# Two fused transformer layers: an order of transposes, late squares, and memory queries without their norm

## What is computed

```python
x = x + rmsnorm(y @ w_out, g_mix_post)
h = rmsnorm(x, g_mem_pre)
q = (h @ w_mq).reshape(B, S, MEM_HEADS, MEM_HEAD_DIM)      # 4 heads of 256
logits = einsum('bshd,bmhd->bhsm', q, k) * MEM_HEAD_DIM ** -0.5
p = softmax(logits); o = einsum('bhsm,bmhd->bshd', p, v)
x = x + rmsnorm(o @ w_mo, g_mem_post)
h = rmsnorm(x, g_ff_pre)
x = x + rmsnorm(square(relu(h @ w_ff1)) @ w_ff2, g_ff_post)
...
qkv = silu(causal_short_conv(g_qkv, conv_w)); gq, gk, gv = split(qkv)
gq = l2_normalize(gq) * 128 ** -0.5; gk = l2_normalize(gk)
o_gdn = gated_delta_rule_chunked(gq, gk, gv, g, beta)
x = x + (sigmoid(gate_a) * o_gdn + sigmoid(gate_b) * o_att) @ w_out_2
h2 = rms_norm(x, norm_mlp_g); x = x + square(relu(h2 @ w_mlp_up)) @ w_mlp_down
```

## Time and profile before

| | us |
|---|---|
| median of 3 runs | 990.76 (990.04 to 992.05) |
| the profiled execution | 989.58 |
| its span from first to last instruction | 987.8 |
| TensorE busy | 944.5 (96%) |
| VectorE busy | 590.7 (60%) |
| ScalarE busy | 526.6 (53%) |
| GpSimd busy | 120.1 (12%) |

### The profile page before, as it was taken

One profiled execution on the slowest core, in us unless ns is written; L12 is line 12 of the kernel. 1 busy time (PEld: TensorE's weight loads), 2 busy tenths in 40 slices (PEclk: granted clock), 3 DMA queues, 4 the chain that ended last, 5 costly groups with the idle time before them and its releaser, 6 DMA issues. The chain is left out here.

```text
span 987.8 us, 15123 instructions
## 1 busy us (share of the span) xinstructions
PE 944.5 (96%) x5920; PEld 831.3 (84%) x5920; DVE 590.7 (60%) x903; ACT 526.6 (53%) x949; POOL 120.1 (12%) x131
## 2 busy tenths in 40 slices
PE   5999999999999999998999998999999999999998
PEld 5996978788889988887779897887899779998886
DVE  4456556753766654446578988776446566665432
ACT  5555666654655453336477686753455364544331
POOL 0020000100100000001014222401654100000000
PEclk9999999999999999999999998999999999999999
DMA  9663423541556655554446443432110064655552
GB/s 339 235 194 129 128 89 126 179 144 41 170 176 191 210 172 197 186 171 171 133 135 203 128 147 110 129 127 86 44 43 2 29 216 150 195 181 174 207 173 85
DMA packets 99702, 146.74 MB, mean 149 GB/s; under 512 B 2480, under 2 KB 57904, under 8 KB 99504
## 3 DMA queue, kind: packets, MB, share of 16 engines
q1 hardware_dynamic: 99632, 145.78, 45.1%
HBM read 144.72 MB, written 1.05 MB: 148 GB/s over the span
## 5 line engine op out<-in xcount | busy, mean ns | idle before, releaser
L396 DVE TENSOR_TENSOR s_w_lo<-s_w_raw,s_w_hi 128x2048 fp32r<-128x2048 f32 (+1 forms) x198 | 313.2, 1599 | 195.7 <-ACT s_w_hi L390 195.7
L390 ACT ACTIVATE s_w_hi<-s_w_raw 128x2048 fp32r<-128x2048 f32 (+1 forms) x198 | 262.6, 1345 | 132.3 <-PE acc L448 103.6
L458 PE MATMUL acc<-s_h_hi,s_w_hi 128*128 128x256 f32 x800 | 228.3, 285 | 6.0 <-DVE s_w_lo L396 4.6
L459 PE MATMUL acc<-s_h_lo,s_w_hi 128*128 128x256 f32 x800 | 226.6, 283 | 0.0
L460 PE MATMUL acc<-s_h_hi,s_w_lo 128*128 128x256 f32 x800 | 226.6, 283 | 0.0
L458 PEld LDWEIGHTS acc<-s_h_hi,s_w_hi 128*128 128x128 f32 x800 | 153.8, 192 | 7.5 <-issue 6.0
L459 PEld LDWEIGHTS acc<-s_h_lo,s_w_hi 128*128 128x128 f32 x800 | 153.9, 192 | 0.1
L460 PEld LDWEIGHTS acc<-s_h_hi,s_w_lo 128*128 128x128 f32 x800 | 153.7, 192 | 0.0
L447 PE MATMUL acc<-s_w_lo,s_hid_hi 128*128 128x512 f32 x224 | 88.5, 395 | 0.0
L448 PE MATMUL acc<-s_w_hi,s_hid_lo 128*128 128x512 f32 x224 | 88.5, 395 | 0.0
L446 PE MATMUL acc<-s_w_hi,s_hid_hi 128*128 128x512 f32 x224 | 88.5, 395 | 0.0
(11 more groups left out here) (320 smaller groups left out, 1587.0 us busy)
## 6 DMA issues: line engine op xcount, KB each, us to landing
s_w_raw<-in_w_in SPq DMA_DIRECT2D x44, 1024.0 KB, 5.2
s_w_raw<-in_w_ff SPq DMA_DIRECT2D x32, 1024.0 KB, 5.2
s_w_raw<-in_w_mlp_up SPq DMA_DIRECT2D x16, 1024.0 KB, 5.3
s_w_raw<-in_w_mlp_down SPq DMA_DIRECT2D x16, 1024.0 KB, 5.0
s_w_raw<-in_w_out SPq DMA_DIRECT2D x8, 1024.0 KB, 5.1
s_w_raw<-in_w_mk SPq DMA_DIRECT2D x4, 1024.0 KB, 5.1
s_w_raw<-in_w_mv SPq DMA_DIRECT2D x4, 1024.0 KB, 5.1
s_w_raw<-in_w_mq SPq DMA_DIRECT2D x4, 1024.0 KB, 5.4
```

The lines of the kernel that those rows point to most:

```text
L390: act.activation(w_hi[u % SPLIT_SLOTS][:, cs], w_raw[u % RAW_SLOTS][:, cs], ACT.Copy).then_inc(w_hi_done, 4 if q is None else 1)
L396: dve.tensor_tensor(w_lo[u % RAW_SLOTS][:, cs], w_raw[u % RAW_SLOTS][:, cs], w_hi[u % SPLIT_SLOTS][:, cs].bitcast(F32), ALU.subtract).then ...
L458: pe.matmul(o, wh[:, cs], hi[:, k, :], start=k == 0, stop=False)
L459: pe.matmul(o, wh[:, cs], lo[:, k, :], start=False, stop=False)
```

## The change

Four parts, in one edit.

- The token transposes go queries, keys, values (`TOK`); each kind waits only for its own qkv units. Gate unit 2 is moved ahead of the value transposes on TensorE, and `gate_tick(6)` (a weight split and two tanh) ahead of their copies on ScalarE. On GpSimd the queries' factors come first, and the keys' factors stand between the last two convolutions. VectorE's first key scaling waits for both sets of factors.
- The squares of x for the norm ahead of layer 1's feed-forward, and those for layer 2's, leave the place ahead of the hidden loop: tile 0's are taken at its step 4, tile 1's at its step 6.
- The turn after the output projection of layer 1 becomes one of the second kind: x is transposed as it is, the queries are made of it without the norm's factor, and that factor becomes the item's "row" in the memory attention. ScalarE takes these four squares behind the copies of the transposed queries and ahead of the evacuation of "mq" unit 2. VectorE waits for both factors before the memory attention.
- Items with a "row" get their 128x1 product by pairs, as one 128x2 product behind the second mask; `l_done` is then raised by two at once.

```diff
-            if pre == "ff":
+            if pre != "mix2":
                 SQUARES += ...
@@ at_dve_mask
-                dve.drain()
-                dve.scalar_tensor_tensor(nmax[:, i:i + 1], nmax[:, i:i + 1], -1.0, it["row"], ALU.mult, ALU.mult).then_inc(l_done, 1)
+                if i % 2:
+                    dve.drain()
+                    dve.scalar_tensor_tensor(nmax[:, i - 1:i + 1], nmax[:, i - 1:i + 1], -1.0, it["rows"], ALU.mult, ALU.mult).then_inc(l_done, 2)
@@ mem_items
+                                      rows=rstd[:, 4 * NCOL["mpre"] + t:4 * NCOL["mpre"] + t + 1].broadcast_to([P, 2]),
+                                      row=rstd[:, 4 * NCOL["mpre"] + t:4 * NCOL["mpre"] + t + 1],
@@ ff_act
-            act.wait_ge(x_done, 2 * NT * 2)
-            for t in range(NT):
-                for g in range(2):
-                    square(act, pre, g, t, x[:, t, g * 512:(g + 1) * 512])
+        def x_squares(act, tag, pre, t):
+            act.wait_ge(x_done, 2 * NT * TURN[tag] + 2 * (t + 1))
+            for g in range(2):
+                square(act, pre, g, t, x[:, t, g * 512:(g + 1) * 512])
@@ hidden_act
             for j in range(16 + 2):
+                if j in (4, 6):
+                    t = j // 2 - 2
+                    if tag == "ff1":
+                        x_squares(act, "mo", "ff", t)
+                    else:
+                        for g in range(2):
+                            wait_added(act, "out2", g, t)
+                            square(act, "mlp2", g, t, x[:, t, g * 512:(g + 1) * 512])
@@
-        TOK = [(kind, n, g) for kind in (1, 0, 2) for n in range(NT) for g in range(2)]
+        TOK = [(kind, n, g) for kind in (0, 1, 2) for n in range(NT) for g in range(2)]
-            pe.wait_ge(qkv_done, {1: 8, 0: 8, 2: 12}[kind])
+            pe.wait_ge(qkv_done, 4 * kind + 4)
@@ tok_scale_dve
             if k == 0:
-                dve.wait_ge(tok_rms, 1)
+                dve.wait_ge(tok_rms, 2)
@@ gpsimd
+            tok_rms_pool(pool, 0)
+            conv_pool(pool, 10)
             tok_rms_pool(pool, 1)
-            conv_pool(pool, 10)
             conv_pool(pool, 11)
-            tok_rms_pool(pool, 0)
@@ scalar
-            turn_act(act, "out", "p_out", "mpre", h_hi)
+            ff_act(act, "out", "p_out", "mpre")
...
             mq_act_tr(act)
+            for t in range(NT):
+                x_squares(act, "out", "mpre", t)
             evacuate(act, "mq", 2)
...
             qkv_act_tanh(act, 11)
+            gate_tick(6)
             act.wait_ge(qkv_done, 12)
             for b in range(8, 12):
                 tok_act(act, b)
-            gate_tick(6)
@@ vector
-            turn_dve(dve, "out", "p_out", "mpre", 1, h_hi, h_lo)
+            ff_dve(dve, "out", "p_out", "mpre", 1)
             for u in of["mq"]:
                 advance_lo(dve, u)
+            for t in range(NT):
+                N.wait(dve, rstd_done)
@@ tensor
-            pair_mm(pe, of["out"][-2], h_hi, h_lo)
-            head_mm("mq")
+            pair_mm(pe, of["out"][-2], h_hi, h_lo, within=lambda t: x_tile("out", 0) if t else None)
+            pair_mm(pe, of["mq"][0], h_hi, h_lo, normed[0], within=lambda t: x_tile("out", 1) if t == 0 else None)
...
                 if b == 7:
-                    mm("ga", 0, 1)
-            mm("ga", 2)
+                    mm("ga", 0, 1, 2)
```

More of the change, by code:

```diff
@@ L872, in dsa_items @@
                                       bias=selb[:, t, 0:nk], row=hrms[:, (AH + AKV) * t + h:(AH + AKV) * t + h + 1],
+                                      rows=hrms[:, (AH + AKV) * t + h // 2 * 2:(AH + AKV) * t + h // 2 * 2 + 2],
                                       v=[av[:, b, kv * AD:(kv + 1) * AD] for b in range(t + 1)],
@@ L1561, in tok_rms_pool @@
         def tok_rms_pool(pool, kind):
-            pool.wait_ge(tok_ss, 8 - 4 * kind)
+            pool.wait_ge(tok_ss, 4 + 4 * kind)
             c = 36 - 16 * kind
@@ L1587, in tok_scale_dve @@
             elif k < 6:
-                dve.wait_ge(tok_rms, 2)
                 dve.tensor_tensor(qh[:, n], qh[:, n], per_head(hrms[:, 36 + 8 * n:44 + 8 * n]), ALU.mult).then_inc(tok_done, 1)
@@ L1949, in _ @@
                     rstd_pool(pool, post, t)
-                    if pre != "ff":
+                    if pre == "mix2":
                         rstd_pool(pool, pre, t)
-                if pre == "ff":
+                if pre != "mix2":
                     for t in range(NT):
-                        r2_pool(pool, pre, t)
+                        {"mpre": rstd_pool, "ff": r2_pool}[pre](pool, pre, t)
             gates2_pool(pool)
@@ L2162, in _ @@
                 gain_act(act, "mlp2", 1, g)
[L2163 to L2166, removed]
             hidden_act(act, "up")
@@ L2407, in x_tile @@
                 for g in range(2):
-                    if tag == "mo":
-                        pe.wait_ge(x_done, 2 * NT + 2 * t + g + 1)
+                    if tag in TURN:
+                        pe.wait_ge(x_done, 2 * NT * TURN[tag] + 2 * t + g + 1)
                     else:
@@ L2467, in _ @@
             tile_mm(pe, u1, 1, h_hi, h_lo, fresh).then_inc(unit_done, 1)
-            pair_mm(pe, of["out"][-2], h_hi, h_lo)
-            head_mm("mq")
+            pair_mm(pe, of["out"][-2], h_hi, h_lo, within=lambda t: x_tile("out", 0) if t else None)
+            pair_mm(pe, of["mq"][0], h_hi, h_lo, normed[0], within=lambda t: x_tile("out", 1) if t == 0 else None)
+            normed[0] += NT * KC
             mm("mq", 2)
```

## The result

The change takes 978.07 us (median of 4 runs, 977.12 to 978.98), the kernel before, run beside it, 990.4. The ratio is 0.9875, with a 95% interval of 0.9854 to 0.9895: 1.2% faster. The forecast was 976.3, in a range of 972.8 to 982. The profiled execution took 977.19 us over a span of 975.4, 12.4 us less than before. Two of the four runs have a mean granted clock of 1.00 and take 977.12 and 977.19 us; the other two have 0.997 and 0.998 and take 978.95 and 978.98.

The account below looks back on a forecast made before the run. TensorE, busy 96% of the span, was taken as the bound, so only its standstills or half clock could be won. 8.35 + 4.7 + 4.9 - 3.5 = 14.5 us gave 976.3 us, range 972.8 to 982.

Parts of the forecast that it names:

- Turn behind the output projection: First matmul to the first one past the turn: 28.57 us becomes 23.83, a gain of 4.7 us.
- Memory attention: It pays for the shorter turn: cost 3.5 us, not less than 1.75, and 5.0 with half clock.
- late mask: Memory attention: squares stand ahead of ScalarE's split and VectorE's low part, so the first mask is 1.75 us late.
- pair gate: Memory attention: `l_done` by pairs makes scores wait for a second mask and a product, 0.85 us for the next pair.
- lower clock that I priced as a rival: Memory attention: the 2.65 us lost leaves half clock, 1.5 us more, 977.8; its chance lies within the forecast's 0.67.
- Hidden loops: Squares leave the place ahead of both loops, so two TensorE waits of 2.44 us go: gain 4.9 us.
- Token stage: Token transposes in the new order: key transposes start at 644.3 instead of 652.65, a gain of 8.35 us.
- a sign of being wrong: Token transposes: a value wait of over 2 us was listed among what would show the forecast wrong.
- if that cover went: Token stage: if GpSimd's last convolution no longer ended ahead of VectorE's turn, values would be late by the excess.
- the value wait stays: Token stage rival: VectorE's run and GpSimd's 3 us hold the values; gain 5.6 instead of 8.35, 979; chance 0.10.
- Sparse attention: Products by pairs there were costed at nothing, between +1 and -2 us.
- The pair gate as the bound: Rival: each of 12 pairs in memory and sparse attention costs about 2.4 us; 11 us slower, 1002; chance 0.04.

Follow-up runs that it names:

- tok_only: Only the token transposes' new order with its waits, gate unit 2, `gate_tick(6)` and GpSimd's order, on the kernel before: 985.39 us, ratio 0.994.
- loops_only: Only the squares of x moved to steps 4 and 6 of the two hidden loops, on the kernel before: 984.6 us, ratio 0.9931.
- sq_early: Full change with the four squares for the memory factors in ScalarE's two gaps ahead of the transposed queries: 976.86 us, ratio 0.9852.
- no_pairs: Full change with one factor product per item again, in memory and sparse attention: 977.24 us, ratio 0.9858.
- best: Full change with conv_first, sq_early and no_pairs together: 971.95 us, ratio 0.9802.
- memq_only: Only the turn behind the output projection, its four squares and products by pairs, on the kernel before: 990.35 us, ratio 0.9987.
- gps_only: Full change with only GpSimd's order altered, last convolution ahead of the key factors: 975.82 us, ratio 0.984.
- lo_quarters: Full change with VectorE's two low parts behind the token sums each computed in four pieces: 977.57 us, ratio 0.9855.
- scale_behind: Full change with only VectorE's order altered, last qkv unit ahead of the first key scaling: 976.85 us, ratio 0.9853.
- conv_first: Full change with the last convolution ahead of the key factors on GpSimd and the last qkv unit ahead of the first key scaling on VectorE: 973.64 us, ratio 0.9823.

## Why the prediction was right or wrong

**Turn behind the output projection: right in size.** From its first matmul to the first one past it, 203.10 - 179.18 = 23.92 us, where 23.83 was forecast; the first memory scores moved by 4.68. The subtraction hid one thing: the 28.57 of before held some lower clock (0.72 from 192 to 198). In tok_only and loops_only, which keep the old turn, the clock is 1.00 there and the first memory scores start at 219.6 instead of 220.16. The structure is worth some 4.1 us, the clock 0.6. That the forecast's 4.7 came out owes these 0.6 us to an old turn that happened to lose its clock in the profile of before.

**Memory attention: right mechanism, over-priced.** Forecast 3.5 us, measured 2.8. The two terms were real, the late mask (1.1 us by sq_early) and the pair gate (0.9 by no_pairs), but with both gone 0.8 us stay (best), so they are 2.0 of the 2.8. The term that was sized wrong is "both masks (0.42 us each) and the product, 0.48 us" with read-outs: the masks followed each other at 0.35 us, the scores being ready, and the product on two columns showed 0.16 us. So the third item's scores came 3.87 us behind the first (219.35 - 215.48) and not 4.39 (224.55 - 220.16), and the next pair's waited 0.33 us and not 0.85. The first mask itself was at 218.19, 2.7 us behind the first scores, against 2.8 forecast. The lower clock that I priced as a rival comes in some executions of a kernel and not in others: in the profiles of memq_only and gps_only, not in that of the change.

**Hidden loops: right.** Both waits are gone, and nothing took their place; the landmarks moved by 2.4 and 2.2 us. What the forecast did not price is that such a wait costs the clock in some executions, where "which the 2.44 us in front of 276.21 did not" was read from a single one.

**Token stage: the step that failed.** Forecast 8.35 us, measured 5.9. The keys are transposed 37.0 us behind the sparse attention's last output (43.0 before), where 35 was forecast, and the 2.80 us of value wait are over the 2 us that the forecast had named as a sign of being wrong. TensorE's side came out: it was at the values at 637.00, which is 641.3 on the clock of before (the sparse attention's last output moved from 609.03 to 604.76), against 641.5. VectorE's side did too: its low part came at 622.00, 1.2 us earlier as forecast. What failed is the sentence "the last convolution on GpSimd waits behind these 3 us and ends near 638.7, ahead of VectorE's turn to use it". It ended at 638.36, or 642.6 on the clock of before, 3.9 us later than forecast. The 3 us were the power alone (2.94). The addition ahead of it took 2.43 us and the convolution 4.10 instead of 3.04, both because VectorE's instructions with two SBUF inputs ran beside them (lo_quarters and scale_behind). GpSimd in the kernel before, where the addition took 0.26 us although short two-input instructions of VectorE (128x256) ran beside it:

```profile
635.23 3.04 POOL L1467 TENSOR_TENSOR s_qkvT<-s_qkvT,s_cprod 128x255 f32<-128x255 f32 x3 [3.35 <-ACT s_cprod L1456]
638.35 0.26 POOL L1568 TENSOR_SCALAR s_hsum<-s_hsum 128x16 f32<-128x16 f32 x1
```

I had made it a condition, "if that cover went, the values would be late by what is over", and the rival "the value wait stays", at 0.10, is what happened, though by GpSimd and not by VectorE's run, which had 1.96 us to spare. It gave 5.6 us and not 8.35, with half clock behind the wait; measured 5.9, with the clock at 1.00. The keys then waited 0.65 us for ScalarE's copies of the values, which I had not costed.

**Sparse attention: right, nothing.** The forecast weighed the Trainium skill (VectorE: DVE Perf Modes, "The DRAIN you can't avoid"), by which fewer chained operations are a gain. no_pairs takes the pairing away, and the stretch stays at 51.4 us: the saved operations were not on the path.

**Sum.** 4.7 + 4.6 - 2.8 + 5.9 = 12.4 us between the two profiles, against 14.5 forecast. The miss is the 2.4 us at the token stage and 0.3 at the hidden loops, less 0.7 in the memory attention. So two errors cancel in part, and the measured 978.07 lies nearer to the rival of the value wait (979) than to the forecast's 976.3. The pair gate as the bound (1002 us) was far off: TensorE waited for a product in the sparse attention for 0.9 us in all.

## What to carry to other kernels

When a wait is removed from the busiest engine, walk the chain of the next one back through every engine, and price GpSimd's steps with what VectorE runs at the same moment. Here the order of two steps on GpSimd and two on VectorE was worth 3.5 us by the profiles, more than the 2.4 that the token stage had missed. Put work without a deadline (factors) behind the work that a waiting engine needs, and small reductions into gaps that the timeline shows ahead of the critical copy. A gate that is raised by pairs saves operations, which is a gain only where that engine is late, and delays the first of each pair: here it cost 0.9 us in the memory attention and gained nothing in the sparse one.

## What the runs showed that was not expected

- A step on 128x16 values on GpSimd took 0.20 us beside VectorE's reductions, which have one SBUF input, 2.43 beside one VectorE subtraction of 2.28 us, and 0.63 beside the same work in quarters. So the length of one VectorE instruction is what such a step waits for. The power was not held like this: 3.15 us beside VectorE's instructions of 631.01 to 635.41, 2.92 at 619.36, where a reduction ran beside its first microsecond. Why the power differs from the addition stays open.
- The same wait of TensorE, of 2.0 to 2.9 us, is followed by the lower clock in some executions and not in others: 2.28 us at the hidden loop left 1.00 in one profile and 0.72 over 6 us in another. It adds 1.2 to 1.4 us in the two places where it was measured. With the waits gone there is less of this: four of five runs of conv_first have a mean clock of 1.00, those of before beside them 0.991 to 0.995.
